# The filler products of TensorE at the four norms are removed

## The reference

```python
mod = silu(c) @ ada_w + ada_b                      # six rows of 2048
h = rms_norm(x, norm1_g) * (1 + sc1) + sh1         # first norm
u = h @ w_in + b_in                                # 2048 -> 4096
a, gt = split(u); u = a * sigmoid(gt)
u = depthwise_conv(u, 31 taps, causal) + b_dw
u = silu(layer_norm(u, ln_g, ln_b))                # layer norm
x = x + g1 * (u @ w_out + b_out)                   # 2048 -> 2048
h = rms_norm(x, norm2_g) * (1 + sc2) + sh2         # second norm
x = x + g2 * (square(relu(h @ w1)) @ w2)           # 2048 -> 8192 -> 2048
return rms_norm(x, final_g)                        # final norm
```

## Time and profile before

| | |
|---|---|
| median of 3 runs | 2015.94 us (2015.42 to 2017.69) |
| profiled execution's own time | 2016.07 us |
| its span, first to last instruction | 2014.2 us |
| TensorE products busy | 1976.3 us (98%), 8659 instructions |
| VectorE / ScalarE / GpSimd busy | 1077.8 / 676.0 / 260.4 us |
| HBM | 299.71 MB moved, 149 GB/s over the span |
| mean granted clock of TensorE | 0.994 of full |
| products of the filler line | 29, the first at 31.4 us, the last at 1999.4 us |

### The profile page before, as it was taken

The page is one execution under the profiler, slowest core; times in us unless marked ns, Lnnn a source line. Parts: engine busy times, 40 slices in busy tenths (PEclk is TensorE's granted clock), DMA queues, the critical chain, the costliest instruction groups (busy, mean ns, idle before and its releaser), DMA issues.

```text
span 2014.2 us, 21615 instructions
## 1 busy us (share of the span) xinstructions
PE 1976.3 (98%) x8659; PEld 1616.3 (80%) x8659; DVE 1077.8 (54%) x1167; ACT 676.0 (34%) x749; POOL 260.4 (13%) x145
## 2 busy tenths in 40 slices
PE   7889999999999999999999999999999999999997
PEld 3668888878878888888888888888888888888886
DVE  6989999978899785233233223322322332332244
ACT  5455545453422422321331232132122223212333
POOL 0009999810000000000000000000000000000001
PEclk8999999999999999999999999999999999999999
DMA  9962322239797475222322222222222222222212
GB/s 392 377 261 105 104 83 105 104 150 366 290 383 285 183 299 193 104 104 83 104 99 89 104 83 104 104 83 104 100 87 104 89 98 99 89 103 87 100 63 84
DMA packets 46120, 299.71 MB, mean 149 GB/s; under 512 B 4737, under 2 KB 4993, under 8 KB 11137
## 3 DMA queue, kind: packets, MB, share of 16 engines
q1 hardware_dynamic: 46082, 299.25, 39.7%
HBM read 295.03 MB, written 4.19 MB: 149 GB/s over the span
## 4 chain that ended last, share of the span: by engine, by line
PE 86%; DVE 10%; issue 1%; ACT 1%; DMA 1%; POOL 0%; SPq 0%; POOLq 0%; DVEq 0%; ACTq 0%
PE ps L420 57%; PE ps L425 28%; DVE raw L985 2%; DVE adar L985 2%; DVE wlo L1007 2%; DVE ps L1071 1%; DMA adar<-ada 1%; DVE hlo L991 0%; DVE quad L1002 0%; ACT xb L857 0%; DVE quad L1016 0%; DVE ada_l L985 0%; DVE ada_h L985 0%; DVE xb L1175 0%; PE ps L501 0%
## 5 line engine op out<-in xcount | busy, mean ns | idle before, releaser
L420 PE MATMUL ps<-hlo,whi 128*128 128x512 f32 (+1 forms) x1792 | 650.2, 389 | 8.8 <-DVE hlo L991 8.8
L420 PE MATMUL ps<-hhi,whi 128*128 128x512 f32 (+1 forms) x1792 | 650.0, 390 | 5.4 <-ACT hhi L684 2.2
L664 ACT ACTIVATE whi<-raw 128x2048 fp32r<-128x2048 f32 x176 | 336.3, 1911 | 635.1 <-PE ps L425 635.1
L425 PE MATMUL ps<-hhi,wlo 128*128 128x512 f32 (+1 forms) x1792 | 435.1, 389 | 0.0
L1007 DVE TENSOR_TENSOR wlo<-raw,whi 128x2048 fp32r<-128x2048 f32 x151 | 346.0, 2292 | 119.8 <-ACT whi L664 119.8
L420 PEld LDWEIGHTS ps<-hlo,whi 128*128 128x128 f32 x1792 | 335.8, 188 | 81.0 <-issue 6.3
L420 PEld LDWEIGHTS ps<-hhi,whi 128*128 128x128 f32 x1792 | 335.4, 188 | 80.6 <-issue 5.7
L420 PE MATMUL ps<-dhi,whi 128*128 128x512 f32 x1024 | 397.0, 389 | 0.0
L420 PE MATMUL ps<-dlo,whi 128*128 128x512 f32 x1024 | 397.0, 389 | 0.0
L425 PEld LDWEIGHTS ps<-hhi,wlo 128*128 128x128 f32 x1792 | 336.3, 188 | 69.9
L1270 DVE SCALAR_TENSOR_TENSOR xb<-ps,modb,xb 128x512 f32<-128x512 f32 x128 | 90.4, 747 | 365.7 <-PE ps L425 356.1
(11 more groups left out here) (148 smaller groups left out, 796.6 us busy)
## 6 DMA issues: line engine op xcount, KB each, us to landing
raw<-w SPq DMA_DIRECT2D x176, 1024.0 KB, 4.8
raw<-ada SPq DMA_DIRECT2D x52, 1024.0 KB, 6.5
adar<-ada SPq DMA_DIRECT2D x36, 1024.0 KB, 7.4
xb<-xT SPq DMA_DIRECT2D x8, 1024.0 KB, 7.8
ada_h<-ada SPq DMA_DIRECT2D x4, 1024.0 KB, 17.9
ada_l<-ada SPq DMA_DIRECT2D x4, 1024.0 KB, 20.8
out<-xb SPq DMA_DIRECT2D x10, 256.0 KB, 2.7
out<-xb SPq DMA_DIRECT2D x3, 512.0 KB, 4.4
```

The source lines that it names most:

```text
L420: return pe.matmul(ps[:, bank, :], whi[:, slot, tile * P:(tile + 1) * P], x, start=first, stop=False, skip_group_check=True)
L425: return pe.matmul(ps[:, bank, :], wlo[:, slot, tile * P:(tile + 1) * P], x, start=False, stop=last, skip_group_check=True)
L664: act.activation(whi[:, q % WS, :], raw_slot(q), ACT.Copy).then_inc(whi_done, 1)
```

## The change

All calls of `keep_busy` and the function are removed; with them go their waits for `whi_done` and one wait for `cs_ready` at the first norm. The other instructions of all engines stay as they are and in the same order.

```diff
--- before.py
+++ after.py
@@ -488,13 +488,6 @@
                                      start=start and j == 0, stop=False, skip_group_check=True)
                 return last
 
-            def keep_busy(n, bank, seen):
-
-                pe.wait_ge(whi_done, seen)
-                for _ in range(n):
-                    pe.matmul(ps[:, bank, :], whi[:, 0, 0:P], whi[:, 0, 0:T], start=True, stop=True,
-                              skip_group_check=True)
-
             def spread(bank, col0):
 
                 for j in range(T // P):
@@ -522,8 +515,6 @@
             pe.wait_ge(root_done, 1)
             spread(7, 8)
 
-            pe.wait_ge(cs_ready, D // T)
-            keep_busy(8, 0, 1)
             pe.wait_ge(rstd_done, 1)
             outer_units(A0, 0, chunk_first=True)
 
@@ -560,7 +551,6 @@
             spread(4, 12)
             pe.wait_ge(root_done, 2)
             spread(2, 8)
-            keep_busy(6, 6, B0 + 1)
             pe.wait_ge(rstd_done, 3)
             outer_units(B0, KC)
 
@@ -575,14 +565,11 @@
 
             pe.wait_ge(ss1_done, KC - 1)
             token_sums(2, 0, ssum, True)
-            keep_busy(2, 5, C0)
             pe.wait_ge(x1sq_done, KC)
             token_sums(2, 0, sig, False).then_inc(stat_done, 1)
-            keep_busy(2, 5, C0)
             pe.wait_ge(root_done, 3)
             spread(3, 8)
 
-            keep_busy(4, 5, C0 + 1)
             pe.wait_ge(rstd_done, 4)
             outer_units(C0, 2 * KC, HIDDEN_ORDER)
 
@@ -645,10 +632,8 @@
 
             pe.wait_ge(ss2_done, KC - 1)
             token_sums(0, 0, ssum, True)
-            keep_busy(3, 3, NUNITS)
             pe.wait_ge(x2sq_done, KC)
             token_sums(0, 0, ta, False).then_inc(stat_done, 1)
-            keep_busy(4, 3, NUNITS)
             pe.wait_ge(root_done, 4)
             spread(1, 8)
             spread(2, 8)
```

## The result

The kernel without fillers takes 2020.89 us (median of 16 executions, 2018.57 to 2022.32); the one before, on the same chips, 2016.84 us (16 executions, 2015.39 to 2017.69). The ratio is 1.0021 with a 95% interval of 1.0014 to 1.0028, which is +4.1 us. Between the two medians lie 4.05 us; forecast were 4.2. The profiled execution took 2020.99 us (span 2019.2, mean clock 0.987 of full) against 2016.07 (2014.2, 0.994).

A forecast was written before the change was run, and what follows sets the result against it. TensorE's stream was taken to bound the kernel (86% of the chain that ended last). First, layer, second and final norm: 0 + 2.0 + 1.9 + 0.3 = +4.2 us, 2020.1 us against 2015.94; range 2017.3 to 2023.0.

The forecast's parts named there:

- The fillers' own time is off the path: All norms: fillers run while TensorE waits, except about 0.1 us regained at the second norm and 0.2 at the final.
- First norm, cost 0: First norm: low clock goes on into real products, but TensorE's waits for VectorE cover it; without cover up to 3.2 us.
- its rival: First norm, rival in that run's own forecast: every low stretch reaching dense products is paid, +2.4 us, ratio 1.0012; no chance given.
- The price of a low stretch: Dense products on TensorE: a low-clock stretch filled with products loses 0.47 of its length.
- Layer norm, +2.0 us: Behind the layer norm: real products run low for 4.2 us, costing 2.0 us (0.6 to 2.5), carried in full.
- Second norm, +1.9 us: Behind the second norm: low products lose 2.0 us, less 0.1 gained, with no later wait to take it up.
- Final norm, +0.3 us: Final norm: 0.5 us taken for a possible clock fall ahead of the spreads, less 0.2 us regained.
- The sum: Whole kernel: the four norms' terms add to +4.2 us, 2020.1 us against 2015.94.
- the fillers never mattered: Rival, both middle norms: clock returns with the spreads, none falls before the final ones; only 0.3 us gained, 2015.6; chance 0.12.
- one norm escapes: Rival, layer or second norm: clock returns early at one, leaving +2.3 us, 2018.2; chance 0.24.
- The Trainium skill's rule on idle gaps: Whole kernel: clock drops come from idle gaps longer than any opened here, so nothing is lost and 0.3 us gained.
- each return comes while fillers run behind a spread: First, layer and second norm: full clock returns (32.9, 418.6, 602.9 us) during these fillers, before the next stage's first real product.

The follow-up runs named there:

- e1: Only the first norm's eight fillers removed from the kernel before; ratio 1.0000 (0.9991 to 1.0009).
- e2: Only the layer norm's six fillers removed from the kernel before; ratio 1.0005 (0.9996 to 1.0014), +1.0 us.
- e12: All fillers of the layer norm and second norm removed from the kernel before, others kept; ratio 1.0013, +2.6 us.
- e8: All fillers behind spreads (8, 6 and 4) removed from the kernel before, those among the token sums kept; ratio 1.0007, +1.4 us.
- e4: Only the final norm's seven fillers removed from the kernel before; ratio 1.0005 (0.9996 to 1.0014), +1.0 us.
- e10: Only the four fillers behind the second norm's spread removed from the kernel before; ratio 1.0004, +0.8 us.
- e3: Only the second norm's eight fillers removed from the kernel before; ratio 1.0016 (1.0007 to 1.0025), +3.2 us.
- e9: Against the kernel before: first norm's eight fillers removed, four added ahead of second norm's first sums, one trimmed at second and final norm each; ratio 0.9998.

## Why the prediction was right

**The fillers' own time is off the path.** Right. At the final norm 0.29 us came back in the profile (0.2 forecast); at the second norm the sums start 0.05 us behind the square (599.61 + 0.63 = 600.24, then 600.29) instead of 0.19, 0.14 us less. Of these, 0.04 reach the spread: ScalarE's root starts 1.09 us behind these sums (601.38) where it started 0.99 behind them (598.87). The forecast was 0.1, so it was a little high.

**First norm, cost 0.** Right: the first group ended at 38.21 us (38.2 forecast), the second group was low in part and late, and later waits took that in, which shrank from 9.9 to 7.9 us. e1 excludes the 2.4 us of its rival; its interval reaches to 1.8.

**The price of a low stretch.** Right: 0.47 of its length forecast; at the layer norm 5.65 us of low products cost 2.69, 0.48.

**Layer norm, +2.0 us.** The mechanism is right and the carrying too: sums of the second norm 2.55 us later, 1.84 in e2. In the profile full clock returns 5.6 us behind the first product, not 4.2, and the term is 2.69 us, a little above the upper end of 2.5. The three other profiles without these fillers have 1.6 us, with 3.3 to 3.4 us of low products; alone it measured +1.0. Over executions, 2.0 is neither confirmed nor refuted. That the low stretch simply goes on was one of at least two ways: in e12 and e8 it began (again) only behind the first product.

**Second norm, +1.9 us.** Loss behind it 2.39 us in the profile, and 0.94 came back in the norm itself, mostly in its spread, which leaves 1.45. I had not counted this gain: I took the low stretch as beginning where it began before. Alone it measured +3.2 us. By how much the size is off stays open; the two numbers lie on both sides of 1.9.

**Final norm, +0.3 us.** Too small: +1.0 us in the profile (-0.29 + 1.03 + 0.3) and +1.0 in e4. VectorE's part was 1.03 us (0.94 forecast for a low spread) and the end, measured from the spread's start, came some 1.3 us later (at most 1.7 forecast); only the weight that I gave to a fall in time was low. The clock fell ahead of the final spreads in all three profiles without these fillers, and never ahead of them in the ten with full-width ones. The term is mis-sized, by some 0.7 us.

**The sum.** +4.2 forecast, +4.1 measured. That they agree so well is in part luck. In the profiled pair the terms are 0, 2.69, 1.45 and 1.04 with 0.14 gained ahead of them, 5.0 us together; the kernels with one norm's fillers removed give 0, 1.0, 3.2 and 1.0, 5.2 us together. I had set it on the three first executions' median of 2015.94; over 16 the kernel before stands at 2016.84, so the absolute 2020.1 is 0.8 low for that reason.

**The rivals.** That the fillers never mattered is excluded by the result. That one norm escapes is not what the changed kernel's profile shows, and all four profiles without the layer norm's fillers lose there; e8 gets nearly all of it back in the norm itself, and a second norm without the four fillers behind its spread escapes in e10. The Trainium skill's rule on idle gaps (TensorE: Matmul & The Clock Gate, section "Why this matters for your kernels"), by which nothing was lost, does not hold here as I applied it: the longest idle of TensorE that the change opens at the two middle norms is 2.45 us, shorter than the gaps that the page names, and the stages behind still ran low. What stood ahead of the idle time, one-column sums and spreads, may count with it; no run separates the two. At the first norm I had overlooked that the change opens a gap of 3.20 us (the row at 34.63), which is as long as those of the page. In the changed kernel the clock was low before that gap already. In e1 the gap is 4.04 us, and the clock fell inside it, at 32.0 us, which agrees with the rule. The loss behind it was covered in both.

**One step was told too simply.** That each return comes while fillers run behind a spread was read as if only these counted, and only by bringing the clock back. e10's profile beside e3's shows that the fillers among the sums ahead of the spread can do a part as well, and e3's beside e12's that fillers behind a spread can also keep a clock that is back.

## What to carry to other kernels

A dip of TensorE's clock at a sync point costs nothing where TensorE is waiting anyway or where another engine bounds the stage behind it, as at the first norm here. It costs where the others wait for TensorE: when dense work that bounds the kernel runs inside it (1.6 to 2.7 us behind the two middle norms), and when a spread on the path does (1.0 us at the final norm). So find each place where light work (sums with one column, small spreads, waits) comes before a dense stage, and cut the profile there into half microseconds, since a page's slices hide it. Fillers in time that is idle anyway are then nearly free (at most 0.3 us here) and earn some 1 to 3 us at each such place. Make them full-width products: with 128 columns in place of 512 the kernel measured +2.4 us here, against +4.1 with none.

## What the runs showed of the hardware

TensorE's clock fell while it issued products without a pause of more than 0.2 us: before the change it ran 32 one-column sums from 410.69 us on and the products of the spreads from 414.43 us on, and the clock fell at 415.2. The moment in a norm at which it changes differs between executions of nearly the same program: at the layer norm the fall was found at 412.1 us (e9), 415.2 (before) and 419.0 (e8, whose two spreads took 2.28 us at full clock), and in e12 a second one at 420.6, among real products. That is a likely reason why executions of one kernel spread over 1.5 to 4.7 us; with one profile of each kernel it is not shown. Whatever the reason, with this spread eleven executions did not settle effects of 1 us, and the lengths of single stages in the profiles did.
